# Where a mixer's transposes and a router's products stand in the order of a two-layer decoder kernel

## The reference

```
for l in range(2):
    h = rmsnorm(x, norm1_g[l]);  x = x + token_mixers(h, ...)
    h = rmsnorm(x, norm2_g[l]);  x = x + hierarchical_moe(h, ...)
return rmsnorm(x, norm_f_g)

# token_mixers: proj = h @ w_in (1024 x 7076), then four branches of width 256
#   y_a  attention on the 64 keys that an indexer picks     y_b  u * (tril(W_s) Norm(v) + b)
#   y_c  stick-breaking attention                           y_d  gated convolution of width 3
merged = sum_n sigmoid(gate_logits[n]) * (y_n @ w_branch[n]);  return merged @ w_out

# hierarchical_moe: top group of 4, then top 2 of its 8 experts
logits = h @ [w_router_group | w_router_expert] + bias        # 4 + 32 columns
return sum over the two experts of weight * (silu(h @ w_g[e]) * (h @ w_u[e])) @ w_d[e]
```

## Time and profile before

| what | value |
|---|---|
| median of 3 runs | 889.68 us (889.56 to 890.39) |
| profiled execution: its time | 889.39 us |
| profiled execution: its span | 887.6 us |
| PE busy | 826.1 us, 93% |
| DVE busy | 529.8 us, 60% |
| ACT busy | 386.5 us, 44% |
| the core's 16 DMA engines | 281.47 MB, 317 GB/s in the mean |

### The profile page before, as it was taken

One profiled execution on the slowest core, in us unless ns is written; L12 is line 12 of the kernel. 1 busy time (PEld: TensorE's weight loads), 2 busy tenths in 40 slices (PEclk: granted clock), 3 DMA queues, 4 the chain that ended last, 5 costly groups with the idle time before them and its releaser, 6 DMA issues.

```text
span 887.6 us, 20367 instructions
## 1 busy us (share of the span) xinstructions
PE 826.1 (93%) x8763; PEld 662.0 (75%) x8763; DVE 529.8 (60%) x1067; ACT 386.5 (44%) x669; POOL 117.3 (13%) x169
## 2 busy tenths in 40 slices
PE   7999999999999998877999999999999999977984
PEld 7898878887897775655589977788789876654652
DVE  5768698667555555423376778976566455534434
ACT  5546868545422222111275568774454222211113
POOL 2840101212000000000066001022200000000000
PEclk9999999999999999978999999999999999999888
DMA  9966545498969999999998463555987999999994
GB/s 305 389 222 160 174 144 188 143 381 322 396 267 418 419 418 420 419 421 420 402 374 294 151 207 123 173 174 222 408 313 282 415 420 420 417 421 419 421 419 183
DMA packets 64125, 281.47 MB, mean 317 GB/s; under 512 B 5120, under 2 KB 7248, under 8 KB 39712
## 3 DMA queue, kind: packets, MB, share of 16 engines
q1 hardware_dynamic: 62752, 278.45, 80.1%
q0 software_dynamic: 800, 1.40, 1.2%
q10 hardware_dynamic: 480, 0.28, 0.1%
HBM read 279.06 MB, written 1.05 MB: 316 GB/s over the span
## 4 chain that ended last, share of the span: by engine, by line
PE 61%; DMA 20%; SPq 6%; issue 5%; ACT 3%; DVE 3%; POOL 1%; DVEq 0%; ACTq 0%; POOLq 0%
PE ps L492 12%; PE ps L494 11%; PE ps L493 11%; DMA ring<-in_w_exp_up 10%; PE ps L825 8%; DMA late<-in_w_exp_down 6%; PE ps L812 5%; PE ps L841 4%; SPq L382 4%; DMA late<-in_w_exp_up 3%; PE ps L925 2%; SPq L396 2%; DMA ring<-in_w_in 2%; POOL wide L1560 1%; PE ps L831 1%
## 5 line engine op out<-in xcount | busy, mean ns | idle before, releaser
L1673 DVE TENSOR_TENSOR split_lo<-ring,split_hi 128x1024 fp32r<-128x1024 f32 (+1 forms) x142 | 196.1, 1417 | 42.0 <-ACT split_hi L1146 40.8
L492 PE MATMUL ps<-split_hi,hT_hi 128*128 128x512 f32 (+2 forms) x416 | 161.4, 388 | 3.1 <-DVE hT_lo L1683 1.4
L1146 ACT ACTIVATE split_hi<-ring 128x1024 fp32r<-128x1024 f32 (+1 forms) x144 | 145.5, 1049 | 29.5 <-PE ps L494 27.3
L493 PE MATMUL ps<-split_lo,hT_hi 128*128 128x512 f32 (+2 forms) x416 | 157.6, 379 | 0.0
L494 PE MATMUL ps<-split_hi,hT_lo 128*128 128x512 f32 (+2 forms) x384 | 145.2, 378 | 0.0
L2085 DVE TENSOR_TENSOR wsT<-mb,ps 32x64 f32<-32x64 f32 x256 | 54.9, 215 | 141.2 <-ACT mb L1356 138.5
L1356 ACT ACTIVATE mb<-ps 128x64 f32<-128x64 f32 x64 | 14.3, 223 | 243.7 <-PE ps L825 243.7
L492 PEld LDWEIGHTS ps<-split_hi,hT_hi 128*128 128x128 f32 x416 | 78.2, 188 | 21.8 <-issue 3.7
L493 PEld LDWEIGHTS ps<-split_lo,hT_hi 128*128 128x128 f32 x416 | 78.3, 188 | 12.9
L494 PEld LDWEIGHTS ps<-split_hi,hT_lo 128*128 128x128 f32 x384 | 72.2, 188 | 13.3
L1577 POOL TENSOR_TENSOR idx<-idx,wt 128x128 f32<-128x128 f32 x32 | 12.1, 399 | 393.8 <-PE ps L847 309.8
(11 more groups left out here) (278 smaller groups left out, 1317.9 us busy)
## 6 DMA issues: line engine op xcount, KB each, us to landing
ring<-in_w_in SPq DMA_DIRECT2D x52, 1024.0 KB, 10.0
ring<-in_w_exp_gate SPq DMA_DIRECT2D x45, 1024.0 KB, 24.5
ring<-in_w_exp_up SPq DMA_DIRECT2D x45, 1024.0 KB, 26.1
late<-in_w_exp_down SPq DMA_DIRECT2D x38, 1024.0 KB, 26.4
ring<-in_w_exp_down SPq DMA_DIRECT2D x15, 1024.0 KB, 26.7
new_pair<-in_w_exp_gate SPq DMA_DIRECT2D x10, 1024.0 KB, 18.6
new_pair<-in_w_exp_up SPq DMA_DIRECT2D x10, 1024.0 KB, 20.9
late<-in_w_exp_gate SPq DMA_DIRECT2D x9, 1024.0 KB, 24.6
```

The lines of the kernel that those rows point to most:

```text
L492: mm(dst, st[0], mv[0], start=start, stop=False, skip_group_check=True)
L493: mm(dst, st[0], mv[1], start=False, stop=False, skip_group_check=True)
L1146: A(half_view(split_hi[:, v % SPLITS, :], v), raw_half(v, l), ACT.Copy).then_inc(hi_done, 1)
L1673: V.tensor_tensor(half_view(split_lo[:, v % SPLITS, :], v), raw_half(v, l), half_view(split_hi[:, v % SPLITS, :], v).bitcast(F32), ALU.sub ...
```

## The change

Six edits, the same in both layers:

1. In unit 16 the twelve transposes of PE stood between half 32 and half 33. They now stand inside half 33, between its products for token tile 0 and those for tile 1, and the four of y_b come first.
2. `pv` for tile 1 stood ahead of `wide_unit(17)` and now stands behind it. The transposes of y_c and the first indexed logits stood ahead of half 36 and now stand behind it.
3. ACT loads the sigmoid table early and does `yT_high` ahead of `token_evac(8)` and `p_evac`. DVE does `yT_low` ahead of `gate(0, 8)`.
4. The wait for `gate_sum` 5 moves from before half 62 to behind it.
5. Unit 35 is multiplied by token tiles: tile 0 whole, tile 1's first 512 columns, half of the rest; then x's transposes, its scaling and the router's products come in turns with what is left. The four idle matmuls go, and DVE does all four scalings.
6. ACT writes the normalized rows of both tiles.

```diff
@@ PE, unit 16 to 18
+                    def second_tile():
+                        pe.wait_ge(*L(yb_done, 1))
+                        y_transposes(y_ab, 6)
+                        pe.wait_ge(*L(zexp, 2))
+                        p_transposes(zc, 1, 4)
+
                     in_half(32, 9)
-                    pe.wait_ge(*L(zexp, 2))
-                    p_transposes(zc, 1, 4)
-                    pe.wait_ge(*L(yb_done, 1))
-                    y_transposes(y_ab, 6)
-                    in_half(33, 9)
+                    in_half(33, 9, "natural", second_tile)
+                    pe.wait_ge(*L(yT_lo_out, 2))
+                    wide_unit(17, 10, y_tile(1), True, True)
                     pe.wait_ge(*L(pT_out, 2))
                     pe.wait_ge(*L(y_out, 1))
                     pv(vc, 1, 7)
-                    pe.wait_ge(*L(yT_lo_out, 2))
-                    wide_unit(17, 10, y_tile(1), True, True)
+                    in_half(36, 12)
                     pe.wait_ge(*L(y_out, 2))
                     y_transposes(y_c, 5)
                     logits(qkT_a, 0, 6, la_mm)
-                    in_unit(18, 12)
+                    in_half(37, 12)
@@ PE, in_half
-                            for dst, st, mv, opens in outs:
+                            for nth, (dst, st, mv, opens) in enumerate(outs):
+                                if nth == 1 and between is not None:
+                                    between()
@@ PE, unit 31
-                    pe.wait_ge(*L(gate_sum, 5))
...
                     in_half(62, 21)
+                    pe.wait_ge(*L(gate_sum, 5))
                     m_transposes(0)
@@ PE, unit 35 and the router (helpers mid_transposes, router_logits, last_product)
-                    wide_unit(35, 22, m_tile(3), False, True)
-                    pe.wait_ge(router_loaded, 16 * 2 * (l + 1))
-                    keep_warm(4, 7)
...
+                    for k in range(2):
+                        pe.wait_ge(*L(lo_done, 2 * NU - 1 + k))
+                        for hf in range(2):
+                            ins = last_product(k, hf, 0)
+                    ins.then_inc(mid_mm, 1)
+                    for k in range(2):
+                        ins = last_product(k, 0, 1)
+                    ins.then_inc(mid_mm, 1)
+                    last_product(0, 1, 1).then_inc(half_used, 1)
+                    pe.wait_ge(*L(x_mid, 1))
+                    mid_transposes(0, 0)
+                    mid_transposes(0, 1)
+                    last_product(1, 1, 1).then_inc(half_used, 1)
+                    pe.wait_ge(router_loaded, 16 * 2 * (l + 1))
+                    router_logits(0, 0)
+                    pe.wait_ge(*L(x_mid, 2))
+                    mid_transposes(1, 0)
+                    router_logits(0, 1)
+                    pe.wait_ge(*L(x_mid, 3))
+                    mid_transposes(1, 1)
+                    router_logits(1, 0)
+                    router_logits(1, 1)
@@ ACT
                     stick_exp(1)
+                    preload_sigmoid()
+                    yT_high(1, 1, 6)
                     token_evac(8, sig, 0, ACT.Sigmoid)
                     p_evac(2, 1, 4)
-                    yT_high(1, 1, 6)
...
-                    act.wait_ge(*L(xT_mm, 13))
-                    for c in range(4, C):
-                        ins = A(hT[:, c, P:2 * P], ps[:, 7, ...], ACT.Copy, scale=g2_col(l, c))
-                    ins.then_inc(xT_hi, 1)
                     act.wait_ge(inv_rms, 2 * l + 2)
-                    A(xnp[0], xp[0], ACT.Copy, scale=ir[:, 0:1]).then_inc(xn_act, 1)
+                    for t in range(TT):
+                        A(xnp[t], xp[t], ACT.Copy, scale=ir[:, t:t + 1]).then_inc(xn_act, 1)
@@ DVE
-                    gate(0, 8)
-                    yT_low(2, 1, 6)
+                    yT_low(2, 1, 6)
+                    gate(0, 8)
...
+                    dve.wait_ge(*L(mid_mm, 1))
+                    mid_add(0, 0)
+                    mid_add(0, 1).then_inc(x_mid, 1)
+                    dve.wait_ge(*L(mid_mm, 2))
+                    mid_add(1, 0).then_inc(x_mid, 1)
+                    mid_scaled(0)
+                    mid_scaled(1)
+                    dve.wait_ge(*L(half_used, 2 * NU))
+                    mid_add(1, 1).then_inc(x_mid, 1)
+                    mid_scaled(2)
+                    mid_scaled(3)
                     inverse_rms(dve, link, 2 * l + 1)
                     dve.wait_ge(inv_rms, 2 * l + 2)
-                    V.tensor_scalar(xnp[1], xp[1], ir[:, 1:2], None, ALU.mult).then_inc(xn_dve, 1)
```

More of the change, by code:

```diff
@@ L103 @@
     conv_y=1, ln_var=1, ln_root=1, vn_dve=1, vn_done=1, sgu_mm=1, yb_done=1, yT_mm=3, yT_hi_out=4, yT_lo_out=4,
-    la_mm=2, la_max=2, la_exp=2, gate_prod=8, gate_sum=6, mid_mm=1, wide_mm=4, x_mid=2,
+    la_mm=2, la_max=2, la_exp=2, gate_prod=8, gate_sum=6, mid_mm=2, wide_mm=4, x_mid=3,
     route_mm=2, gmax=1, gexp=1, emax=1, eexp=1, member_ok=1,
@@ L424, in preload_sqrt, with preload_sigmoid @@
             nc.scalar.activation(spare, eps_t[:], ACT.Sqrt)
+        def preload_sigmoid():
+            nc.scalar.activation(spare, eps_t[:], ACT.Sigmoid)
         def preload_gelu():
@@ L560, in wide_unit @@
                             pe.wait_ge(*L(lo_done, v + 1))
[L561 to L565, removed]
+                            for n, (hf, t) in enumerate((hf, t) for hf in range(2) for t in range(TT)):
                                 if first_ and v % 2 == 0 and t == 0:
@@ L569, in wide_unit @@
                                             first_ and v % 2 == 0, last_ and v % 2 == 1)
-                                if final_half and n == 1:
-                                    ins.then_inc(mid_mm, 1)
-                                elif first_ and last_ and v % 2 == 1 and n == 1:
+                                if first_ and last_ and v % 2 == 1 and n == 1:
                                     ins.then_inc(wide_mm, 1)
@@ L787, in _, with last_product, mid_transposes @@
[L787 to L790, removed]
+                    def last_product(k, hf, t):
+                        return three(ps[:, 2 * hf + t, :], m_tile(3)(k, t), w_tile(2 * NU - 2 + k, 0, 512 * hf, 512),
+                                     False, k == 1)
+                    def mid_transposes(t, q):
+                        for c in range(4 * q, 4 * q + 4):
+                            ins = nc.tensor.transpose(ps[:, 4 + 2 * t + q, P * (c % 4):P * (c % 4) + P],
+                                                      x[:, t, P * c:P * c + P], ident[:])
+                        ins.then_inc(xT_mm, 1)
@@ L791, in _, with router_logits @@
+                    def router_logits(t, q):
+                        pe.wait_ge(*(L(xT_lo, 10), L(xT_lo, 11), L(xT_lo, 12), L(xT_lo, 13))[2 * t + q])
+                        for c in range(4 * q, 4 * q + 4):
                             ins = mm(ps[:, t, 0:NG + NE], hT[:, c, P * t:P * t + P], wr[:, c, :],
                                      start=(c == 0), stop=(c == C - 1), skip_group_check=True)
-                        ins.then_inc(route_mm, 1)
+                        if q == 1:
+                            ins.then_inc(route_mm, 1)
@@ L852, in gather_group @@
                         if g == 0:
[L853 to L854 removed]
+                            pe.wait_ge(*L(xn_act, 2))
                         if g >= 3:
@@ L1332, in _ @@
                     hi(35)
[L1335 removed]
                     preload_sqrt()
                     for t in range(TT):
[L1339 removed]
+                        act.wait_ge(*L(x_mid, 2 * t + 1))
                         square_of_x(t)
                     root_of_mean(act, 2 * l + 1)
[L1342 to L1345 removed]
                     act.wait_ge(inv_rms, 2 * l + 2)
[L1347 removed]
+                    for t in range(TT):
+                        A(xnp[t], xp[t], ACT.Copy, scale=ir[:, t:t + 1]).then_inc(xn_act, 1)
                     act.wait_ge(*L(gmax, 1))
@@ L1969, in _, with mid_add, mid_scaled @@
                     lo(35)
-                    for t in range(TT):
-                        dve.wait_ge(*(L(mid_mm, 1), L(half_used, 2 * NU))[t])
-                        for hf in range(2):
-                            xs = x[:, t, 512 * hf:512 * hf + 512]
-                            ins = V.tensor_tensor(xs, xs, bank(2 * hf + t), ALU.add)
-                        ins.then_inc(x_mid, 1)
                     V.memset(rt[:, 96:112], -TAKEN)
-                    dve.wait_ge(gain_out, 1)
-                    for k in range(3):
+                    def mid_add(t, hf):
+                        xs = x[:, t, 512 * hf:512 * hf + 512]
+                        return V.tensor_tensor(xs, xs, bank(2 * hf + t), ALU.add)
+                    def mid_scaled(k):
                         t, c0 = k // 2, 4 * (k % 2)
```

18 lines of the change are left out of this document (4 added, 14 removed).

## The result

| what | before | after |
|---|---|---|
| median | 889.61 us (888.78 to 890.39, 6 runs) | 911.34 us (910.63 to 913.08, 6 runs) |
| ratio to before, 95% interval | 1 | 1.0248 [1.0235, 1.0261] |
| span of the profiled execution | 887.6 us | 910.6 us |
| mean granted TensorE clock | 0.972 | 0.961 |

The change makes the kernel slower by 21.7 us. I had predicted 906, within 897 to 914: the direction and the range held, and the time is 5 us above the sum. It lies where the prediction had its rival on the clock (909 to 913, chance 20%), not at the sum that had 62%.

The account below looks back on a forecast made before the run. PE was taken to bound the mixers and bytes the experts, with mixer time counted in full. Per layer 9.2 - 0.6 - 0.5 = +8.1, two layers +16.2, so 906 us for the median, range 897 to 914.

Parts of the forecast that it names:

- rival on the clock: Clock halves behind new waits before halves 33 and 36: +3.4 to +6.8 us in all, 909 to 913; chance 20%.
- the sum that had 62%: All terms together: +8.1 us per layer, +16.2 for two layers, 906 us for the median; chance 62%.
- What bounds it, and that mixer time counts in full: PE's time bounds mixers, bytes bound experts; mixer time won or lost counts at full value in both layers.
- Unit 16, +1.4: Half 33 still starts at 115.51, waiting for DVE's low parts; the transposes lose their cover, +1.4 us on PE.
- Unit 17, a wait of 1.1 for `token_evac(9)`: In `wide_unit(17)`, after its first six matmuls, PE waits 1.1 us because ACT comes late.
- Unit 18, the wait of 3.8: DVE's copy waits for `pv` ahead of half 36's low part, so PE idles 3.8 us before half 36.
- DVE 9.2 us late, paid in full: `yT_low(3)` starts at 136.1 instead of 126.91; PE pays all 9.2 us per layer, lower end +5.
- the link to half 43: DVE has no gap until half 43's low part and PE hangs directly on it, so both are 9.2 us late.
- Unit 31 and the router, -1.1 per layer: End of the mixer: the wait for POOL's addition goes, -0.6 us; the router's new order brings -0.5 us.
- the wait of 0.4 us: In unit 35 PE waits about 0.4 us for the first scaling, since only one product covers it.
- just covered: The norm's chain, 1.2 us of small DVE operations behind the fourth scaling, ends at 240.9, before the logits' read-out near 241.1.
- The exponentials' table load: ACT's exponentials behind the router come about 2.5 us later, costing at most 0.3 us; 1.38 us of draining not counted.

Follow-up runs that it names:

- Edits 1 and 3 alone: Kernel before with the transposes inside half 33 and ACT's and DVE's new order, `pv` and y_c's transposes where they were: 895.19 us, 1.0070.
- edit 2 alone: Kernel before with `pv` behind unit 17 and y_c's transposes behind half 36, the twelve transposes left between halves 32 and 33: 908.94 us, 1.0220.
- the kernel of edits 1 to 3: Kernel before with the edits in units 16 to 18 alone, units 31 and 35 and the router as before: 915.22 us, 1.0290.

## Why the prediction was right, and where its size was off

**What bounds it, and that mixer time counts in full: right.** The gather of layer 1 is 23.03 us late and the last operation 23.04. Layer 0's experts even added 1.0, where I had nothing: the half clock behind a DMA wait that had grown from 1.20 to 2.53 us.

**Unit 16, +1.4: right.** Half 33 at 115.48, the transposes behind its sixth matmul, and the wait is 2.81. Edits 1 and 3 alone make DVE's `yT_low(3)` 2.2 us late per layer (129.02 for 126.91, in an execution that runs 0.12 us early): this 1.4, and 0.5 that `pv` waits for ACT. The rest of their 5.5 us, 1.0, comes in layer 1's experts.

**Unit 17, a wait of 1.1 for `token_evac(9)`: right in size.** 1.2 in layer 1 and 1.21 with idle matmuls. In layer 0 only 0.25 was left, since the transposes ran at the half clock and took up the rest.

**Unit 18, the wait of 3.8: right.** 3.83 in both layers, with the copy waiting for `pv` in front of it. It was named by reading what stands between the copy and the low parts, and confirmed from both sides (edit 2 alone brings it, moving the copy removes it).

**DVE 9.2 us late, paid in full: right within half a us, 9.65 at clock 1.00.** And the link to half 43 held: 12.21 at `yT_low(3)`, 12.20 at half 43.

**The clock: the mis-sized term.** The sum took it as nothing and put it into a rival with 20%. It fell: at half 36 in both layers, and behind the wait before half 33 in both. Taken together it made 12.2 and 13.5 of 9.65, so 6.4 us in the profiled execution, and with the 1.0 in the experts 7.4, above the 3.4 to 6.8 that I gave that rival. A fall at half 36 was priced at 1.7 us, from a low stretch of 3.4 us; the stretch was 6.8 us long, and half 36 took 4.8 us (133.07 to 137.85) in layer 0 and 5.3 in layer 1 in place of 2.8, so 2.0 and 2.5 more. What failed was weighing it: I set the 1.4 us waits that had no fall against it, though my own sum contained a wait of 3.8 us, next to a row with a fall behind 3.94. The Trainium skill ("TensorE: Matmul & The Clock Gate", HAM oscillation) describes idle gaps that throttle the next products. The traces agree: of six waits of 3.8 us without idle matmuls all six were followed by the half clock. They also have it behind shorter waits, down to 2.0 us. That the time still fell into the range is because its upper end had been drawn for two falls per layer.

**Unit 31 and the router, -1.1 per layer: direction right, small by half.** The traces give -2.0 and -1.6, so -3.6 beside -2.2. Unit 31 was taken at the 0.6 us of idling in the list and brings 0.95: at the transposes behind half 62 the lateness has gone from 12.20 to 11.25. The router brings 1.1 in layer 0 and 0.65 in layer 1 in place of 0.5. 0.3 of layer 0's is no gain of the new order: it is the half clock in the router's products of the kernel before, which I had read at their 3.8 us as if that were their full speed. PE wins the whole of its idle matmuls, 0.9 us, because the wait of 0.4 us did not come: PE's transposes and products follow each other from 245.59 on without idling. That PE would still end last, the norm's chain "just covered", was wrong by a little: the read-out follows the norm's last step at once (251.57, 251.77). Edit 6, which I had priced only by what it does on ACT, takes DVE's 1.16 us off this chain.

**The exponentials' table load.** It is followed by its exponential after 1.29 us, as before (255.98 and 257.27). The page that I had weighed, the Trainium skill's "ScalarE: Activation LUTs" (What ACT_TABLE_LOAD costs), adds 1.38 us of draining; no trace here shows it.

Put together from the trace: 2 x 9.65 + 6.4 - 3.6 + 1.0 = 23.1, the difference of the spans is 23.0. The medians are 21.7 apart, since both numbers here are of one execution each.

## What to carry to other kernels

Before an operation is moved down one engine's order, look up in every other engine's order what waits for it, and what is queued behind that waiter: here one 0.42 us copy, left in its place, held up low parts that had nothing to do with it, and moving it along wins back 12 of 22 us. When a sum contains a new idle time on TensorE of 2 us or more, add what the clock takes behind it to the sum itself: in these mixers 17 of 22 such waits had a fall behind them, and none of the shorter ones. Before a row's length goes into a sum, look at its granted clock too. And a chain that is "just covered" by another is to be counted as a second end: it decides as soon as the first one shrinks.

## What the runs showed of the hardware

- The half clock behind a wait of PE, over all twelve traces (the mixers behind their start-up, and layer 0's experts from 440 us on): after 3.8 us in 6 of 6 cases, after 2.8 us in 6 of 10, after 2.5 us in 2 of 2, after 2.0 to 2.1 us in 3 of 4, after 1.1 to 1.8 us in none of 38, and after 3.8 us filled with 15 idle matmuls in none of 4. The same kernel could differ between its layers (in the kernel of edits 1 to 3 none behind the 2.8 us of layer 0, one in layer 1). Behind the waits of 3.8 us the stretch lasted 6.8 us, its first part still within the wait, and behind the others 3.4.
- It also came without a wait: at the end of the mixer, in the router's products or the idle matmuls behind them, in 6 of the 24 ends of mixers in the twelve traces, PE having worked on without idling (before, layer 0: 5.76 us busy of 5.76 in front of the fall).
- In such a stretch a 512-column matmul comes every 0.43 us and not every 0.23. When the waits are filled, DVE's lateness in layer 0 goes from 12.2 to 9.65 us.
- The first product behind a wait takes 0.34 us to the next one in place of 0.23 (115.48 to 115.82), which is part of why a wait listed at 0.60 us cost 0.95.
- DVE's `split_lo` takes 3.44 us behind the start of POOL's addition and 1.22 without it. It ends 1.1 us after the addition does (147.84 and 146.72), as if it had run only then. The Trainium skill ("GPSIMD Engine Reference", Specifications) has the two share their interfaces to SBUF, with contention where a DVE instruction has two SBUF inputs, as this one; the trace agrees. In the prediction it was what tied half 43 to DVE.
